# Six turns instead of eight for a head pair's attention, in a hybrid decoder layer on one core

## The chip, the cores and the metric

The kernel runs on one core of one Trainium2 chip. The metric is the device time of one execution in microseconds; the median of several runs is compared.

## The reference

One decoder layer for 1024 tokens of width 1024. The part that the change touches is the attention group: 8 heads of 64, "stick-breaking" attention, strictly causal.

```python
for blk in range(S // Q_BLOCK):              # eight tiles of 128 queries
    t0 = blk * Q_BLOCK
    L = t0 + Q_BLOCK                         # a tile looks at the keys before its end
    z = jnp.einsum('bhqd,bhkd->bhqk', qb, kb) * scale
    mask = s_idx < t_idx
    log_keep = jnp.where(mask, jax.nn.log_sigmoid(-z), 0.0)
    shifted = jnp.concatenate([log_keep[..., 1:], jnp.zeros_like(log_keep[..., :1])], axis=-1)
    suffix = lax.cumsum(shifted, axis=3, reverse=True)
    A = jnp.where(mask, jnp.exp(jax.nn.log_sigmoid(z) + suffix), 0.0)
    outs.append(jnp.einsum('bhqk,bhkd->bhqd', A, vb).astype(v.dtype))
```

Around it: an RMS norm and a projection to six blocks of 512 columns (b, c, h of a gated causal convolution, and q, k, v), a norm of q and k by head, a norm of both groups' outputs by head, the output projection, and a hierarchical mixture of 32 experts.

## The kernel before

Every engine has its own program, in which the order of all work is written out by hand, and semaphores join them.

Attention runs over four pairs of heads. For a pair the eight query tiles are gone through from the last (tile 7, 1024 keys) to the first (tile 0, 128 keys), one tile a *turn* for both heads: 32 turns, counted by n, and r is the turn within its pair. In iteration n of its loop (L495 to L509) TensorE does `scores(n + 1)`, `values(n - 1)`, `turn(n, 0)`, projection steps, `turn(n, 1)`, projection steps.

- `scores` (L442) multiplies q by k in three products of rounded and remaining parts into z, in banks 0 to 3 (two for each head, used in turn; `z_first`, `z_done` and the semaphore `z_read` say when one may be written again).
- ScalarE's `open_unit` (L587) reads z twice through a sigmoid: `kept` (1 - beta, L597) and `soft` (beta, L598).
- VectorE's `weigh` (L736) makes the running product of `kept` from the right with a scan (L744) and multiplies `soft` by it (L747).
- `turn` (L459) transposes `soft` in blocks of 128 into banks 4 and 5, ScalarE's `take_turned` (L600) copies these out to `probsT` (L606), and `values` (L469) multiplies them by v into bank 6, where four tiles share a bank that `take_values` (L609) copies out.

Between these, TensorE works off the projection of the chunks of columns of q, k, b, c and h, in *steps*: one matmul of 128x128 by 512 (L417). A group of 24 steps makes 512 tokens of one chunk. The first eight groups come ahead of attention; the others are handed out by `share(n)`, so many steps between the two heads' transposes and so many behind the second. All these groups are made in bank 7, and the first step of one waits until the group before has been read (L412). The readers are `take(g)` of ScalarE for k (a square L544 and a copy L545), of ScalarE and then VectorE for q (L549, L550 and L699), and of VectorE for c, h and b (L703, L708, L719). On VectorE `take` stands at the beginning of an iteration, for the groups that ended in the second part of turn n - 1 and the first of turn n, ahead of `weigh(n + 1, 0)`; on ScalarE at the beginning too, for the groups of turn n - 1. `chunk_lo` (L685) on VectorE makes the remaining part of the next weights.

In turn r = JOIN the pair stops for sums of squares: TensorE's `sums_of_qk` and `sums_of_rows` (L421, L435) write them to z banks, ScalarE changes its function table, takes logarithms and exponentials (`roots_of_qk`, `roots_of_rows`) and changes it back; one turn later VectorE scales with them (`scale_keys`, `keys_lo`, `scale_rows`).

Of the kernel before, what the change touches and what calls it, by code (L numbers as in the profile page):

```python
# [19 lines left out]
ALU = mybir.AluOpType  # L20
ACT = mybir.ActivationFunctionType
AX = mybir.AxisListType

P = 128
# [14 lines left out]

SHARE = ((8, 16),) * 8  # L40
SHARE_LAST = ((24, 24),) * 4 + ((0, 0),) * 4


def hymba_moe_layer(nc, x, norm_mix_w, w_in, conv_w, q_norm_w, k_norm_w, group_norm_conv_w,
# [33 lines left out]
    with ExitStack() as ctx:  # L78
# [162 lines left out]
        NPAIR = CB  # L241
        UNITS = NPAIR * NT
        PRE_GROUPS = 2 * PRE


        def share(n):
            return (SHARE if n < UNITS - NT else SHARE_LAST)[n % NT]

# [22 lines left out]
        for n in range(UNITS):  # L271
            z_first[n], z_before[n] = len(z_done), z_done[-1]
            z_done += [z_done[-1] + 2 * halves(n)] * halves(n)
            p, r = divmod(n - 1, NT)
# [10 lines left out]
        assert all(z_first[n] % 2 == 0 for n in range(UNITS) if halves(n) == 2)  # L285

# [9 lines left out]
        with nc.Block(no_gpsimd_drain=True) as block:  # L296
# [82 lines left out]
            def _(pe):  # L379
# [62 lines left out]
                def scores(n):  # L442

                    p, t = n // NT, tile_of(n)
                    cols = slice(t * P, (t + 1) * P)
                    if n % NT == 0:
                        pe.wait_ge(k_ready, p + 1)
                    q2, k2 = (q_hi[p % 2], q_lo[p % 2]), (k_hi[p % 2], k_lo[p % 2])
                    for hf in range(halves(n)):
                        c0, c1 = hf * BANK, min((hf + 1) * BANK, length(n))  # L450
                        pe.wait_ge(z_read, z_done[z_first[n] + hf - 2])
                        for i, (qs, ks) in enumerate(((0, 0), (0, 1), (1, 0))):
                            for h in range(2):
                                rows = slice(h * HD, (h + 1) * HD)
                                mm = pe.matmul(Z(z_first[n] + hf, h)[:, 0:c1 - c0], q2[qs][rows, cols], k2[ks][rows, c0:c1],
                                               start=(i == 0), stop=(i == 2))
                    mm.then_inc(scored, 1)

                def turn(n, h):  # L459
                    pe.wait_ge(weighed, 2 * n + h + 1)  # L460
                    for hf in range(halves(n)):
# [3 lines left out]
                        for j in range(4 * hf, min(4 * hf + 4, length(n) // P)):  # L465
                            mm = pe.transpose(TB(g)[:, (j % 4) * P:(j % 4 + 1) * P], soft[h][:, S - length(n) + j * P:S - length(n) + (j + 1) * P], ident)  # L466
                        mm.then_inc(turned, 1)

                def values(n):  # L469

                    p, t = n // NT, tile_of(n)
                    pe.wait_ge(turned_read, th(n + 1, 0))
                    if n == 0:
                        pe.wait_ge(bank_read[0], PRE)
                    elif n % 4 == 0:
                        pe.wait_ge(out_read, n // 4)
                    for j in range(t + 1):
                        for h in range(2):
                            head = slice((2 * p + h) * HD, (2 * p + h + 1) * HD)
                            mm = pe.matmul(ps[h * HD:(h + 1) * HD, VB, (t % 4) * P:(t % 4 + 1) * P], v[:, j, head], probsT[h][:, j, :],  # L480
                                           start=(j == 0), stop=(j == t))
                    mm.then_inc(valued, 1)
# [12 lines left out]
                for n in range(UNITS):  # L495
                    p, r = divmod(n, NT)
# [12 lines left out]
                    project(ticks_by(n, 1), ticks_by(n, 2))  # L509
# [3 lines left out]
            def _(act):  # L513
# [19 lines left out]
                def take(g):  # L533
# [7 lines left out]
                    if kind == "k":  # L541
                        if h == 0 and j >= 2:
                            act.wait_ge(scored, NT * (j - 1))
                        act.activation(k_sq[j % 2][:, half], o, ACT.Square).then_inc(k_squared, 1)  # L544
# [28 lines left out]
                def square_row(p, i):  # L573
# [3 lines left out]
                    if p == NPAIR - 1:  # L577
                        act.wait_ge(scored, NT * p)
                        act.wait_ge(k_scaled, NPAIR)
# [7 lines left out]
                def open_unit(n, h):  # L587
                    p, t, L = n // NT, tile_of(n), length(n)
                    act.wait_ge(scored, n + 1)
                    if n % NT == 0:  # L590
# [3 lines left out]
                    up, down = q_scale[p % 2][:, t, h:h + 1], q_minus[p % 2][:, t, h:h + 1]  # L594
                    b = 2 * h + z_first[n] % 2
                    z = psf[:, b * BANK:b * BANK + L]
                    act.activation(kept[h][:, S - L:], z, ACT.Sigmoid, scale=down).then_inc(kept_made, 1)  # L597
                    act.activation(soft[h][:, S - L:S - 1], z[:, 0:L - 1], ACT.Sigmoid, scale=up).then_inc(z_read, halves(n))  # L598

                def take_turned(n, h):  # L600
                    for hf in range(halves(n)):
# [3 lines left out]
                        k0, k1 = 4 * hf, min(4 * hf + 4, length(n) // P)  # L605
                        act.activation(probsT[h][:, k0:k1, :], TB(th(n, h) + hf)[:, 0:(k1 - k0) * P].rearrange("p (k t) -> p k t", t=P),  # L606
                                       ACT.Copy).then_inc(turned_read, 1)

                def take_values(i):  # L609

                    act.wait_ge(valued, 4 * i + 4)
                    if i == 2 * (NPAIR - 1):
# [26 lines left out]
                for n in range(UNITS):  # L639
                    p, r = divmod(n, NT)  # L640
                    if n:
# [6 lines left out]
                    for h in range(2):  # L648
                        take_turned(n, h)
                        if n + 1 < UNITS:  # L650
                            open_unit(n + 1, h)
                    if n and n % 4 == 0:
                        take_values(n // 4 - 1)
                    if r == JOIN[p]:
# [5 lines left out]
                        table(2)  # L660
                take_values(UNITS // 4 - 1)

            @block.vector
            def _(dve):
# [71 lines left out]
                def weigh(n, h):  # L736

                    L = length(n)
                    s, k, one = soft[h][:, S - L:], kept[h][:, S - L:], start_at[:, S - L:]
                    if n == 0:  # L740
                        dve.wait_ge(soft_ends, 2)
                    dve.wait_ge(kept_made, 2 * n + h + 1)
                    back = k[:, ::-1]
                    dve.tensor_tensor_scan(back, back, one[:, ::-1], 0.0, ALU.mult, ALU.max).then_inc(multiplied, 1)  # L744
                    dve.wait_ge(multiplied, 2 * n + h + 1)
# [38 lines left out]
                for n in range(UNITS):  # L784
                    p, r = divmod(n, NT)
                    if n:
# [806 lines left out]
```

## Time and profile before

| what | value |
| --- | --- |
| median of 3 runs | 1246.56 us (1245.02 to 1247.19) |
| the profiled execution | 1245.32 us, span 1243.6 us |
| TensorE matmul busy | 1114.1 us (90%) |
| TensorE weight load busy | 909.2 us (73%) |
| VectorE busy | 876.5 us (70%) |
| ScalarE busy | 723.9 us (58%) |
| GpSimd busy | 143.0 us (12%) |
| mean granted clock of TensorE | 0.946 of full speed |

Attention runs from 114.9 us (its first scores) to 445.5 us (the last copy of its values). Behind it come the output projection, the routing and, from 630 us, the experts. In the rows further on, a time is counted from the span's start, "x12" is the number of instructions merged into a row, and the brackets tell how long the engine was idle before and what ended that. PE is TensorE, DVE VectorE, ACT ScalarE.

### The profile page before, as it was taken

How to read it: one execution, taken by the hardware profiler on the slowest of the kernel's cores; microseconds unless marked ns; L12 is line 12 of the kernel's file. 1: busy time of each engine (PE TensorE's matmuls, PEld its weight loads, DVE VectorE, ACT ScalarE, POOL GpSimd, SP SyncE). 2: the span in 40 equal slices, each digit the busy share in tenths (PEclk: the TensorE clock that was granted, in tenths of full speed). 3: DMA queues.
4: the chain of work that ended last, by engine and by line, in shares of the span. 5: the costliest groups of instructions: out<-in, count | busy, mean ns of one | idle time of the engine just before them, and what ended most of it. 6: DMA issues, size and time to landing. Idle time of an engine off the chain costs nothing. (4 is left out here: it accounts for less than half of the span.)

```text
span 1243.6 us, 16698 instructions
## 1 busy us (share of the span) xinstructions
PE 1114.1 (90%) x5806; PEld 909.2 (73%) x5806; DVE 876.5 (70%) x918; ACT 723.9 (58%) x890; POOL 143.0 (12%) x193
## 2 busy tenths in 40 slices
PE   5998999999999869993589999999999999999920
PEld 4886777778778548883378888888888888888810
DVE  4405657576574563225579999999999999999816
ACT  4422655746633532111378888888888888888800
POOL 1001000000000310000101111111111111111000
PEclk9999999999999979995599999999999999999965
DMA  6111010110011362006279999999999999999219
GB/s 205 55 34 35 18 34 18 34 35 19 23 34 30 136 248 90 35 34 280 100 279 371 373 392 393 377 380 389 387 381 379 387 385 381 384 382 387 96 35 387
DMA packets 57338, 261.88 MB, mean 211 GB/s; under 512 B 13008, under 2 KB 33488, under 8 KB 43984
## 3 DMA queue, kind: packets, MB, share of 16 engines
q1 hardware_dynamic: 46928, 240.31, 50.7%
q0 software_dynamic: 9216, 16.80, 3.6%
q10 hardware_dynamic: 1152, 4.19, 0.8%
q8 instruction: 28, 0.46, 0.2%
q14 instruction: 14, 0.11, 0.0%
HBM read 252.88 MB, written 25.17 MB: 224 GB/s over the span
## 5 line engine op out<-in xcount | busy, mean ns | idle before, releaser
L1265 DVE TENSOR_TENSOR e_lo<-W,e_hi 128x1024 fp32r<-128x1024 f32 x384 | 452.6, 1221 | 25.8 <-ACT e_hi L1259 23.0
L1259 ACT ACTIVATE e_hi<-W 128x1024 fp32r<-128x1024 f32 x384 | 403.3, 1060 | 97.0 <-PE ps L1230 97.0
L1228 PE MATMUL ps<-e_hi,xT_hi 128*128 128x512 f32 x512 | 204.4, 399 | 7.1 <-DVE e_lo L1265 7.1
L1230 PE MATMUL ps<-e_lo,xT_hi 128*128 128x512 f32 x512 | 201.6, 394 | 0.0
L1229 PE MATMUL ps<-e_hi,xT_lo 128*128 128x512 f32 x512 | 201.0, 393 | 0.0
L744 DVE TENSOR_TENSOR_SCAN kept<-kept,start_at 128x1024 f32<-128x1024 f32 (+7 forms) x64 | 91.2, 1425 | 65.3 <-ACT kept L597 65.3
L417 PE MATMUL ps<-xnT_hi,w_hi 128*128 128x512 f32 x320 | 128.4, 401 | 2.4 <-DVE y_mix L719 0.9
L417 PE MATMUL ps<-xnT_hi,w_lo 128*128 128x512 f32 x320 | 128.1, 400 | 0.0
L417 PE MATMUL ps<-xnT_lo,w_hi 128*128 128x512 f32 x320 | 125.0, 391 | 0.0
L606 ACT ACTIVATE probsT<-ps 128x512 f32<-128x512 f32 (+3 forms) x96 | 43.8, 491 | 128.9 <-PE ps L466 128.8
L1228 PEld LDWEIGHTS ps<-e_hi,xT_hi 128*128 128x128 f32 x512 | 97.6, 191 | 27.0 <-issue 4.0
L1230 PEld LDWEIGHTS ps<-e_lo,xT_hi 128*128 128x128 f32 x512 | 97.0, 190 | 21.0
L1229 PEld LDWEIGHTS ps<-e_hi,xT_lo 128*128 128x128 f32 x512 | 97.4, 190 | 19.4
L1228 PE MATMUL ps<-e_hi,hidT_hi 128*128 128x512 f32 x256 | 103.1, 403 | 2.7 <-DVE e_lo L1265 2.7
L1230 PE MATMUL ps<-e_lo,hidT_hi 128*128 128x512 f32 x256 | 100.4, 392 | 0.0
L1229 PE MATMUL ps<-e_hi,hidT_lo 128*128 128x512 f32 x256 | 100.4, 392 | 0.0
L1322 POOL DMA_INDIRECT y_rows<-y,idx_pair x32 | 32.6, 1020 | 458.5 <-ACT y L1285 458.5
L417 PEld LDWEIGHTS ps<-xnT_hi,w_hi 128*128 128x128 f32 x320 | 60.5, 189 | 15.7 <-issue 3.6
L417 PEld LDWEIGHTS ps<-xnT_hi,w_lo 128*128 128x128 f32 x320 | 60.2, 188 | 13.1 <-issue 0.7
L417 PEld LDWEIGHTS ps<-xnT_lo,w_hi 128*128 128x128 f32 x320 | 60.3, 189 | 12.1 <-issue 0.2
L361 POOL CAST w_hi<-w_raw 128x1024 fp32r<-128x1024 f32 x20 | 23.5, 1176 | 320.6 <-DMA w_raw<-in_w_in_dram 320.6
L1228 PEld LDWEIGHTS ps<-e_hi,hidT_hi 128*128 128x128 f32 x256 | 48.6, 190 | 12.1 <-issue 2.9
(211 smaller groups left out, 1670.6 us busy)
## 6 DMA issues: line engine op xcount, KB each, us to landing
W<-in_w_dram SPq DMA_DIRECT2D x96, 2048.0 KB, 10.3
w_raw<-in_w_in_dram SPq DMA_DIRECT2D x20, 512.0 KB, 4.0
yy<-y_rows SPq DMA_DIRECT2D x8, 1024.0 KB, 13.5
xt<-in_x_dram SPq DMA_DIRECT2D x8, 512.0 KB, 3.7
w_out_raw<-in_w_out_dram SPq DMA_DIRECT2D x4, 1024.0 KB, 8.0
xn_rows<-xn SPq DMA_DIRECT2D x8, 512.0 KB, 2.6
out_dram<-x ACTq DMA_DIRECT2D x8, 512.0 KB, 8.9
x<-in_x_dram SPq DMA_DIRECT2D x1, 3072.0 KB, 14.9
```

The lines of the kernel that those rows point to most:

```text
L361: pool.tensor_copy(w_hi[c % 2], w_raw[c % 2]).then_inc(w_hi_made, 1)
L417: mm = pe.matmul(ps[:, group_bank(g)], w, r, start=(i % TICKS == 0), stop=(i % TICKS == TICKS - 1))
L606: act.activation(probsT[h][:, k0:k1, :], TB(th(n, h) + hf)[:, 0:(k1 - k0) * P].rearrange("p (k t) -> p k t", t=P), ACT.Copy).then_inc(turn ...
L744: dve.tensor_tensor_scan(back, back, one[:, ::-1], 0.0, ALU.mult, ALU.max).then_inc(multiplied, 1)
L1228: pe.matmul(o, xs_hi[:, k], e_hi[:, p, cols], start=(k == 0), stop=False)
L1229: pe.matmul(o, xs_lo[:, k], e_hi[:, p, cols], start=False, stop=False)
L1230: mm = pe.matmul(o, xs_hi[:, k], e_lo[:, p, cols], start=False, stop=(k == last))
L1259: act.activation(e_hi[:, p], flat[:, p * D:(p + 1) * D], ACT.Copy).then_inc(s["hi_made"], 1)
L1265: dve.tensor_tensor(e_lo[:, p], flat[:, p * D:(p + 1) * D], e_hi[:, p], ALU.subtract).then_inc(s["lo_made"], 1)
L1322: pool.indirect_dma_start(out=y_rows, out_offset=bass.IndirectOffsetOnAxis(ap=idx_pair[b].bitcast(U32), axis=0), in_=y[b], in_offset=None, ...
```

## The change

The constants and the turns. Tiles 7, 6, 5 and 4 keep a turn each; tiles 3 and 2 share one, and so do 1 and 0. A turn takes 12 + 20 projection steps in place of 8 + 16; in the last pair the first four turns take 24 + 24 and the others none, as before.

```diff
-SHARE = ((8, 16),) * 8
-SHARE_LAST = ((24, 24),) * 4 + ((0, 0),) * 4
+TURNS = ((7,), (6,), (5,), (4,), (3, 2), (1, 0))
+SHARE = ((12, 20),) * 6
+SHARE_LAST = ((24, 24),) * 4 + ((0, 0),) * 2
@@
-        UNITS = NPAIR * NT
+        NU = len(TURNS)
+        UNITS = NPAIR * NU
@@
-        JOIN = (4, 4, 4, 5)
-        tile_of = lambda n: NT - 1 - n % NT
-        length = lambda n: (tile_of(n) + 1) * P
-        halves = lambda n: (length(n) + BANK - 1) // BANK
+        JOIN = (3, 3, 3, 4)
+        tiles_of = lambda n: TURNS[n % NU]
+        length = lambda t: (t + 1) * P
+        halves = lambda n: 2
+        def parts(n):
+            tiles = tiles_of(n)
+            if len(tiles) == 1:
+                t = tiles[0]
+                return ((t, 0, BANK, S - length(t), 0), (t, BANK, length(t), S - length(t) + BANK, 4))
+            return ((tiles[0], 0, length(tiles[0]), S - length(tiles[0]), 0), (tiles[1], 0, length(tiles[1]), S - BANK - length(tiles[1]), 4))
```

`parts(n)` gives the two parts of a turn: the halves of one tile, or its two tiles. The second tile of a shared turn lies in the other z bank and in the lower half of `soft`, `kept` and `probsT`. `scores`, `turn`, `values` and `take_turned` go over these parts. ScalarE opens both tiles, the two `kept` first, and reads a group that ends in the first part of turn n between the two heads:

```diff
+                    for i, t in enumerate(tiles):
+                        end, L = S - i * BANK, length(t)
+                        b = 2 * h + (z_first[n] + i) % 2
+                        act.activation(kept[h][:, end - L:end], psf[:, b * BANK:b * BANK + L], ACT.Sigmoid,
+                                       scale=q_minus[p % 2][:, t, h:h + 1]).then_inc(kept_made, 1)
+                    for i, t in enumerate(tiles):
+                        end, L = S - i * BANK, length(t)
+                        b = 2 * h + (z_first[n] + i) % 2
+                        act.activation(soft[h][:, end - L:end - 1], psf[:, b * BANK:b * BANK + L - 1], ACT.Sigmoid,
+                                       scale=q_scale[p % 2][:, t, h:h + 1]).then_inc(z_read, 2 // len(tiles))
@@
                         take_turned(n, h)
                         if n + 1 < UNITS:
                             open_unit(n + 1, h)
-                    if n and n % 4 == 0:
-                        take_values(n // 4 - 1)
+                        if h == 0:
+                            for g in groups_in(n, 0):
+                                take(g)
+                    if n and r in (0, 4):
+                        take_values(2 * p + r // 4 - 1)
```

VectorE's `weigh` makes the scans of both tiles, clears the last column of the second tile and multiplies both. The order of its loop stays.

```diff
+                    for i, t in enumerate(tiles):
+                        end, L = S - i * BANK, length(t)
+                        dve.wait_ge(kept_made, scans(n, h) + i + 1)
+                        back = kept[h][:, end - L:end][:, ::-1]
+                        dve.tensor_tensor_scan(back, back, start_at[:, S - L:][:, ::-1], 0.0, ALU.mult, ALU.max).then_inc(multiplied, 1)
+                    dve.wait_ge(multiplied, scans(n, h) + len(tiles))
                     dve.wait_ge(z_read, z_reads(n, h))
-                    dve.tensor_tensor(s[:, :L - 1], s[:, :L - 1], k[:, 1:], ALU.mult).then_inc(weighed, 1)
+                    if len(tiles) == 2:
+                        dve.memset(soft[h][:, S - BANK - 1:S - BANK], 0.0)
+                    for i, t in enumerate(tiles):
+                        end, L = S - i * BANK, length(t)
+                        ins = dve.tensor_tensor(soft[h][:, end - L:end - 1], soft[h][:, end - L:end - 1], kept[h][:, end - L + 1:end], ALU.mult)
+                    ins.then_inc(weighed, 1)
```

All other lines of the diff put the new count of turns (NU for NT) into waits on `scored`, `valued` and `out_read`.

## Rows read from the trace of the kernel before

**Rows 1.** Granted TensorE clock in 40 slices of the span, in tenths, from the page.
```profile
PEclk9999999999999979995599999999999999999965
```
**Rows 2.** Busy time by stretch: start:end length, PE, PEld, DVE, ACT, POOL, clock, DMA share, GB/s.
```profile
132.88:207.71 74.83, 74.12 (x501) 58.76 (x501) 44.56 (x46) 41.53 (x73) 5.61 (x5) 1.00 0.10 29
365.27:417.80 52.53, 52.15 (x321) 42.00 (x320) 30.04 (x28) 18.43 (x31) 2.07 (x2) 1.00 0.07 21
417.80:449.67 31.87, 15.62 (x111) 9.10 (x111) 18.36 (x19) 21.23 (x36) 13.06 (x10) 0.79 0.43 158
```
**Rows 3.** Waits of TensorE's matmuls, 127 to 417 us: us in total, times, longest.
```profile
PE ps L417 <- DVE y_mix L719: 0.9, 2, 0.7
...
PE ps L466 <- DVE soft L747: 0.5, 1, 0.5
```
**Rows 4.** Timeline of TensorE in tile 1's turn: start us, us, engine, line.
```profile
183.67 0.48 PE L417 MATMUL ps<-xnT_hi,w_hi 128*128 128x512 f32 x1
...
185.61 0.38 PE L466 MATMUL ps<-start_at,soft 128*128 128x128 f32 x2
185.75 0.48 PE L417 MATMUL ps<-xnT_hi,w_lo 128*128 128x512 f32 x1
...
189.03 0.39 PE L417 MATMUL ps<-xnT_lo,w_hi 128*128 128x512 f32 x1
189.26 0.39 PE L417 MATMUL ps<-xnT_hi,w_lo 128*128 128x512 f32 x1
189.58 0.50 PE L455 MATMUL ps<-k_hi,q_hi 64*128 64x512 f32 x2
```
**Rows 5.** Timeline, first pair's second turn, from the second head's transposes on.
```profile
138.69 0.93 PE L466 MATMUL ps<-start_at,soft 128*128 128x128 f32 x7
...
139.37 0.47 PE L417 MATMUL ps<-xnT_hi,w_lo 128*128 128x512 f32 x1
...
140.97 0.92 ACT L598 ACTIVATE soft<-ps,q_scale 128x767 f32<-128x767 f32 x1
...
143.30 0.60 ACT L544 ACTIVATE k_sq<-ps 128x512 f32<-128x512 f32 x1 [1.41 <-PE ps L417]
...
143.80 0.59 ACT L545 ACTIVATE k_new<-ps 128x512 f32<-128x512 f32 x1
```
**Rows 6.** Timeline, VectorE's part in reading a query group.
```profile
229.17 0.69 DVE L699 TENSOR_TENSOR q_lo<-ps,q_hi 128x512 fp32r<-128x512 f32 x1 [0.23 <-ACT q_hi L550]
```
**Rows 7.** Timeline, a read of VectorE and the next group's first step.
```profile
380.60 0.69 DVE L703 COPY u<-ps 128x512 f32<-128x512 f32 x1 [7.53 <-PE ps L417]
...
381.34 0.50 PE L417 MATMUL ps<-xnT_hi,w_hi 128*128 128x512 f32 x1
```
**Rows 8.** Timeline, the last sigmoid ahead of the first pair's sums of squares.
```profile
168.02 0.58 ACT L598 ACTIVATE soft<-ps,q_scale 128x383 f32<-128x383 f32 x1
...
168.74 1.96 PE L433 MATMUL ps<-k_sq,same_head 128*128 128x512 f32 x4
```
**Rows 9.** Timeline of all engines in the tail, 423.5 to 445.2 us.
```profile
423.99 1.09 PE L480 MATMUL ps<-probsT,v 128*64 128x128 f32 x16 [2.65 <-ACT y_mix L615]
...
437.62 0.38 ACT L606 ACTIVATE probsT<-ps 128x256 f32<-128x256 f32 x1
...
438.97 1.28 DVE L734 SCALAR_TENSOR_TENSOR y_mix<-y_mix,gain_attn,k_new 128x1024 f32<-128x1024 f32 x1
...
442.55 0.42 DVE L744 TENSOR_TENSOR_SCAN kept<-kept,start_at 128x128 f32<-128x128 f32 x1
...
444.93 0.60 ACT L615 ACTIVATE y_mix<-ps 128x512 f32<-128x512 f32 x1 [0.79 <-PE ps L480]
```
**Rows 10.** Timeline of TensorE, its first matmul behind two idle times.
```profile
120.78 0.80 PE L455 MATMUL ps<-k_hi,q_hi 64*128 64x512 f32 x2 [4.22 <-ACT soft L598]
...
1184.48 0.76 PE L1228 MATMUL ps<-e_hi,hidT_hi 128*128 128x512 f32 x1 [2.73 <-DVE e_lo L1265]
```
**Rows 11.** Busy time by stretch, one behind the second of these idle times.
```profile
1184.20:1187.40 3.20, 2.92 (x7) 2.37 (x8) 3.20 (x4) 0.00 (x0) 1.31 (x2) 0.50 0.22 83
```

More of the change, by code:

```diff
@@ L241, in hymba_moe_layer @@
         NPAIR = CB
-        UNITS = NPAIR * NT
+        NU = len(TURNS)
+        UNITS = NPAIR * NU
+        assert sum(TURNS, ()) == tuple(range(NT - 1, -1, -1)) and all(t < 4 for tiles in TURNS for t in tiles[1:])
         PRE_GROUPS = 2 * PRE
         def share(n):
-            return (SHARE if n < UNITS - NT else SHARE_LAST)[n % NT]
+            return (SHARE if n < UNITS - NU else SHARE_LAST)[n % NU]
         def ticks_by(n, part):
@@ L273, in hymba_moe_layer @@
             z_done += [z_done[-1] + 2 * halves(n)] * halves(n)
-            p, r = divmod(n - 1, NT)
+            p, r = divmod(n - 1, NU)
             if n and r == JOIN[p]:
@@ L284, in hymba_moe_layer @@
         z_reads = lambda n, h: z_before[n] + (h + 1) * halves(n)
-        assert all(z_first[n] % 2 == 0 for n in range(UNITS) if halves(n) == 2)
+        assert all(z_first[n] % 2 == 0 for n in range(UNITS) if len(tiles_of(n)) == 1)
+        scans = lambda n, h: sum(2 * len(tiles_of(m)) for m in range(n)) + h * len(tiles_of(n))
         th = lambda n, h: sum(2 * halves(m) for m in range(n)) + h * halves(n)
@@ L442, in scores @@
                 def scores(n):
-                    p, t = n // NT, tile_of(n)
-                    cols = slice(t * P, (t + 1) * P)
-                    if n % NT == 0:
+                    p = n // NU
+                    if n % NU == 0:
                         pe.wait_ge(k_ready, p + 1)
                     q2, k2 = (q_hi[p % 2], q_lo[p % 2]), (k_hi[p % 2], k_lo[p % 2])
-                    for hf in range(halves(n)):
-                        c0, c1 = hf * BANK, min((hf + 1) * BANK, length(n))
+                    for hf, (t, c0, c1, at0, j0) in enumerate(parts(n)):
+                        cols = slice(t * P, (t + 1) * P)
                         pe.wait_ge(z_read, z_done[z_first[n] + hf - 2])
@@ L460, in turn @@
                     pe.wait_ge(weighed, 2 * n + h + 1)
-                    for hf in range(halves(n)):
+                    for hf, (t, c0, c1, at0, j0) in enumerate(parts(n)):
                         g = th(n, h) + hf
@@ L464, in turn @@
                             pe.wait_ge(turned_read, g - 1)
-                        for j in range(4 * hf, min(4 * hf + 4, length(n) // P)):
-                            mm = pe.transpose(TB(g)[:, (j % 4) * P:(j % 4 + 1) * P], soft[h][:, S - length(n) + j * P:S - length(n) + (j + 1) * P], ident)
+                        for j in range((c1 - c0) // P):
+                            mm = pe.transpose(TB(g)[:, j * P:(j + 1) * P], soft[h][:, at0 + j * P:at0 + (j + 1) * P], ident)
                         mm.then_inc(turned, 1)
                 def values(n):
-                    p, t = n // NT, tile_of(n)
+                    p, r = divmod(n, NU)
                     pe.wait_ge(turned_read, th(n + 1, 0))
@@ L474, in values @@
                         pe.wait_ge(bank_read[0], PRE)
[L475 to L481, printed above, removed]
+                    elif r in (0, 4):
+                        pe.wait_ge(out_read, 2 * p + r // 4)
+                    for i, t in enumerate(tiles_of(n)):
+                        for j in range(t + 1):
+                            for h in range(2):
+                                head = slice((2 * p + h) * HD, (2 * p + h + 1) * HD)
+                                mm = pe.matmul(ps[h * HD:(h + 1) * HD, VB, (t % 4) * P:(t % 4 + 1) * P], v[:, j, head], probsT[h][:, 4 * i + j, :],
+                                               start=(j == 0), stop=(j == t))
                     mm.then_inc(valued, 1)
@@ L495, in _ @@
                 for n in range(UNITS):
-                    p, r = divmod(n, NT)
+                    p, r = divmod(n, NU)
                     if n + 1 < UNITS:
@@ L542, in take @@
                         if h == 0 and j >= 2:
-                            act.wait_ge(scored, NT * (j - 1))
+                            act.wait_ge(scored, NU * (j - 1))
                         act.activation(k_sq[j % 2][:, half], o, ACT.Square).then_inc(k_squared, 1)
@@ L577, in square_row @@
                     if p == NPAIR - 1:
-                        act.wait_ge(scored, NT * p)
+                        act.wait_ge(scored, NU * p)
                         act.wait_ge(k_scaled, NPAIR)
@@ L587, in open_unit @@
                 def open_unit(n, h):
-                    p, t, L = n // NT, tile_of(n), length(n)
+                    p, tiles = n // NU, tiles_of(n)
                     act.wait_ge(scored, n + 1)
-                    if n % NT == 0:
+                    if n % NU == 0:
                         act.wait_ge(q_minus_made, p + 1)
@@ L593, in open_unit @@
                         act.wait_ge(turned, th(n - 1, h) + halves(n - 1))
[L594 to L598, printed above, removed]
+                    for i, t in enumerate(tiles):
[8 more added lines that the diff above has]
+                                       scale=q_scale[p % 2][:, t, h:h + 1]).then_inc(z_read, 2 // len(tiles))
                 def take_turned(n, h):
-                    for hf in range(halves(n)):
+                    for hf, (t, c0, c1, at0, j0) in enumerate(parts(n)):
                         act.wait_ge(turned, th(n, h) + hf + 1)
@@ L639, in _ @@
                 for n in range(UNITS):
-                    p, r = divmod(n, NT)
+                    p, r = divmod(n, NU)
                     if n:
@@ L660, in _ @@
                         table(2)
-                take_values(UNITS // 4 - 1)
+                take_values(2 * NPAIR - 1)
             @block.vector
@@ L736, in weigh @@
                 def weigh(n, h):
-                    L = length(n)
-                    s, k, one = soft[h][:, S - L:], kept[h][:, S - L:], start_at[:, S - L:]
+                    tiles = tiles_of(n)
                     if n == 0:
                         dve.wait_ge(soft_ends, 2)
[L742 to L745, printed above, removed]
-                    dve.wait_ge(z_read, z_reads(n, h))
-                    dve.tensor_tensor(s[:, :L - 1], s[:, :L - 1], k[:, 1:], ALU.mult).then_inc(weighed, 1)
+                    for i, t in enumerate(tiles):
[4 more added lines that the diff above has]
+                    dve.wait_ge(multiplied, scans(n, h) + len(tiles))
+                    dve.wait_ge(z_read, z_reads(n, h))
+                    if len(tiles) == 2:
[4 more added lines that the diff above has]
+                    ins.then_inc(weighed, 1)
                 dve.wait_ge(g1_in, 16)
@@ L784, in _ @@
                 for n in range(UNITS):
-                    p, r = divmod(n, NT)
+                    p, r = divmod(n, NU)
                     if n:
```

5 lines of the change are left out of this document (2 added, 3 removed).

## The prediction

> **What bounds the kernel now.** I read the page's slices first: apart from its two ends and the middle, TensorE is at 9 tenths at the full clock [rows 1]. The table by stretch then splits the attention stage by head pair: in the first pair TensorE is busy 74.12 of 74.83 us, in the last pair's four big tiles 52.15 of 52.53, but in the 31.87 us behind them only 15.62 [rows 2]. The waits say the same: between 127 and 417 us TensorE waits on L417 0.9 us for the largest releaser, and the four kinds of wait add up to 2.8 us [rows 3]. So three stretches matter: three pairs and most of a fourth that are bound by TensorE's own instructions, and a tail of 32 us that is bound by a chain through ScalarE and VectorE. What follows (projection out, routing, experts) is not touched.
>
> A change of the turns can therefore gain in the dense part only by fewer TensorE switches; it can gain in the tail; and it can lose wherever it makes TensorE wait. The last is what decides it.
>
> **What is the same.** All matmuls, transposes, activations and scans keep their number and sizes: a merged turn makes the scans of tiles 3 and 2 (or 1 and 0) one after the other. The 960 projection steps are also the same. Added are 16 one-column memsets on VectorE. No row shows one; the nearest is a scan over 128 columns, 0.42 us (442.55, [rows 9]), so each costs between 0 and 0.42. I take 0.1; they lie on a chain only for group 6 below.
>
> **Fewer turns in the dense part: a gain.** A step is repeated every 0.23 us (189.03 to 189.26). Eight steps take 1.94 us (183.67 to 185.61) and sixteen 3.83 (185.75 to 189.58) [rows 4], which is 8 and 16 times 0.227 and 0.12 and 0.20 over. So a change from one kind of work to another costs TensorE 0.1 to 0.2 us. A turn has six kinds of work in a row (scores, values, transposes, steps, transposes, steps), and for all but the transposes the change goes with the turn: 4 x 0.14, so I take 0.55 us for a turn removed, bounds 0.3 and 1.0. Two turns in each of three pairs: -3.3 us.
>
> **Where the groups of 24 steps end: the loss.** All groups from 8 on are made in one PSUM bank (group_bank gives 7), and the first step of a group waits until ScalarE or VectorE has read the bank of the group before. Before, a turn is 8 + 16 = 24 steps, so each group ends with its turn, and the next turn's scores, values and transposes hide the reading. Now a turn is 12 + 20 = 32 steps. The sums in a pair run 12, 32, 44, 64, 76, 96, 108, 128, 140, 160, 172, 192, and the groups end at 24, 48, 72, 96, 120, 144, 168, 192. Only 96 and 192 are ends of a turn. The six others lie inside a block of steps, with nothing between them and the next group. In the walk below X is the start of the transposes of the second head in the turn named.
>
> A bare VectorE read: the last step ends at 380.56, the copy runs 380.60 to 381.29 and TensorE goes on at 381.34 [rows 7]. So the next step starts 0.39 + 0.78 = 1.17 us after the last one did, in place of 0.23: 0.95 us. A key group (square, copy: 143.30 to 144.39, [rows 5]) costs in the same way 0.39 + 0.04 + 1.09 + 0.06 - 0.23 = 1.35. A query group has VectorE's subtraction behind the same two (229.17, 0.69 us and 0.1 behind ScalarE, [rows 6]): 0.39 + 0.04 + 1.88 + 0.06 - 0.23 = 2.15.
>
> - Group 1 (keys, ends 12 steps into the 20 of the first turn): ScalarE has done its turn by then, 1.35 (1.5 in later pairs, where the copy of the values comes first).
> - Group 2 (keys, 4 steps into the 20 of the second turn). ScalarE reads it only behind taking the transposes and opening the next unit. In this very turn before, X is 138.69, the second sigmoid ends at 141.89 = X + 3.2 [rows 5]; the group is read by X + 4.2. TensorE would go on at X + 0.68 (139.37) + 0.12 + 4 x 0.227 = X + 1.7. Loss 2.5.
> - Group 3 (queries, 8 steps into the 12 of the third turn): 2.15; ScalarE comes to it in time, 8 steps after the first head's transposes.
> - The sums of squares. They now follow a merged turn's opening, whose z uses two banks, and wait for its last reading. Before, only their second part (168.74) had to wait for the sigmoid of 168.02, which ended at 168.60, and the first part ran beside it [rows 8]. Now the whole opening counts. The nearest row is again [rows 5]: a copy of 896 columns and two sigmoids of 768 end at X + 3.2. Here it is a copy of 640, then 2 x 896 in two instructions more: about X + 3.5, where TensorE has only five transposes, 0.46. Loss 3.05, bounds 2 and 4.
> - Group 5 (VectorE's, 12 steps behind the sums): bare, 0.95.
> - Group 6 (VectorE's, 4 steps into the 20 of turn (3, 2)). VectorE must first finish weigh for turn (1, 0). It comes to it at about X + 2.2, behind keys_lo and chunk_lo (each as large as one scale_rows, 1.19 [rows 9]), of which the first starts when the first head's weigh is done, near X. Its sigmoids end at X + 2.85: those of [rows 5] less 2 x 384 columns at 0.9 ns (768 columns take 0.92, 384 take 0.58 [rows 8]) and two instructions more. A scan of 128 takes 0.42, so both take 1.2 and both products 0.8 with the memset: X + 4.2, and the read of 0.69 X + 4.9, where TensorE stands at X + 1.7. Loss 3.2; in the second and third pairs scale_rows lies ahead too, 2 x 1.19 (438.97 to 442.55 is three of them, [rows 9]): 5.6.
> - Group 7 (8 steps into the 12 of turn (1, 0)): bare, 0.95.
> - The group that ends the pair is now read in time, since the turn ahead of it has 12 + 20 steps: -0.66, the wait of before for L703 or L708, one per pair.
>
> First pair: 1.35 + 2.5 + 2.15 + 3.05 + 0.95 + 3.2 + 0.95 = 14.15, less 0.66: 13.5. The second and third have 0.15 + 2.4 more: 16.05 each. Together 45.6 us, and with the 3.3 us of fewer turns +42.3. Of the first pair's waits, 0.5 us of L466 for VectorE [rows 3] goes, since four more steps stand before it: +41.8. The fourth pair's 24 + 24 are kept, so its groups end with blocks as before.
>
> **The tail: a gain.** Counting from the last step's end at 417.8, the last copy starts at 444.93 and ends at 27.7 [rows 9]. Now, with the same durations set in the new order: the last group is read by 0.7, the last row squared by 1.9; four copies (0.4 to 0.6 each) and turn (1, 0)'s eight sigmoids (0.25 to 0.36 each from start to start) end at 7.0; the three rows' sums start there (two z banks again), and their logarithms, exponentials and the two tables take ScalarE to 17.4 (it was 437.62 - 417.8 = 19.8). Behind it stand only: two copies, the second head's three transposes, two copies, 12 values (0.9), one copy of 0.6. That ends at 20.7. The three scale_rows on VectorE, which stood ahead of the last weigh (438.97 to 442.55), now lie beside this. 27.7 - 20.7 = 7.0, less 0.5 for two tiles' scores ahead of the last steps: -6.5, bounds -4 and -9. Where the second block's first matmuls start sooner they may find a lower clock for longer; I keep that in the bounds.
>
> **The clock.** TensorE fell to 0.50 (1.2 GHz) after an idle of 4.22 us (matmul at 120.78, 0.80 us long in place of 0.50) and after one of 2.73 (at 1184.48), where 1184.20 to 1187.40 is at 0.50 [rows 10, 11]; an idle of 2.65 (at 423.99) was followed by 1.00 up to 424 and beyond [rows 1, 9]. The new idles of 3.05, 3.2 and 5.6 us are on the side that falls, those of 2.5 and 2.15 on the line or below it. I take two falls a pair. In 3.2 us at half clock about 3 us of dense work loses 1.5 us; the longer stretch after 120.78 lost about 2.5. Six falls at 1.7: +10 us, bounds 0 and 22. The Trainium skill, in "TensorE: Matmul & The Clock Gate" (HAM oscillation), says that a kernel whose matmul bursts are separated by waits is put back to half rate at each burst anew; by it every larger gap of a pair would be followed by a fall. The trace agrees behind 2.73 us (0.50, [rows 11]) and not behind 2.65.
>
> **Sum.** 41.8 - 6.5 + 10 = +45.3 us. The profiled execution took 1245.32 us (span 1243.6 and 1.7 around it), 1.24 below the median, so it would give 1290.6; against the median, 1292.
>
> **Rivals.**
> 1. No clock falls, the waits as walked: +35.3, 1282. For it: the idle of 2.65 us that did not fall. Chance 0.14.
> 2. The longer waits are covered, only the bare handoffs are paid: two keys 2.7, queries 2.15, three of VectorE's 2.85 are 7.7 a pair, less 0.66 and 1.1: 3 x 5.9 - 6.5 = +11, 1258. It needs ScalarE and VectorE to reach the reads earlier than their program order lets them; [rows 5] speak against it. Up to 1270: chance 0.10.
> 3. The clock falls at every wait over 2 us, and stays down longer: four or five falls a pair at 1.7 to 2.5 are 22 to 37 in place of 10: 1304 to 1319. Chance 0.08, since five such falls a pair would need the idles of 2.15 to fall where 2.65 did not. It is what the section of the Trainium skill named above would give.
> 4. The other side: the tail and the fewer turns win. They bring 6.5 + 3.3 + 2.0 (three times 0.66) = 11.8 us, 1235. This decides if the seven new waits of a pair cost under 3.9 us together, 0.56 each; the smallest read in the trace costs 0.95. It would hold if the groups' readers did not gate the next group, which the code's one bank excludes. Chance 0.02, and 0.02 for no change.
>
> **Numbers.** Forecast 1292 with its own 1285 to 1301: chance 0.64. The range reaches from 1270 to 1303; it leaves out rival 2, 3 and 4. What a measurement can tell from no change is about 0.2%, 2.5 us. Faster 0.02, same 0.02, slower 0.96.
>
> **What would show it.** In the changed trace the waits list TensorE's L417 waiting behind ScalarE's key copy and VectorE's reads, some 35 us more in three pairs, up to about 5 us at once; within a block of 12 or 20 steps a hole at the group's end; the matmul behind the sums' start waiting for a sigmoid; a table by pair with 11 to 20 us more for each of three pairs, the fourth's four tiles unchanged, a tail of 21 in place of 28 us; granted clock under 1.00 in each pair. It is wrong if the holes inside the blocks are missing, if they stay at a microsecond each (rival 2), or if the clock stays at 1.00 (rival 1).

## The result, and the profile after

The changed kernel takes 1299.81 us (median of 5 runs, 1298.29 to 1301.61) where the kernel before takes 1246.56: a ratio of 1.043 (95% interval 1.0415 to 1.0444), +53 us. The forecast was 1292 with a range from 1270 to 1303, slower. The two profiled spans are 1296.6 and 1243.6 us, so all of the difference can be read in them.

In the changed kernel a projection step is L429, the scores are L466, the transposes L477, the values L492, and the sums of squares L439 (queries) and L452 (rows). Of the readers, L556 and L557 are ScalarE's for keys, L718 is VectorE's part of a query group, and L722, L727 and L738 are VectorE's for c, h and b; L614 is ScalarE's sigmoid `soft`. In the variants with six turns these lines are up to ten further on.

The table by stretch first. In the changed kernel the stretches begin with the first scores behind TensorE's idle time of 4.22 us, with the end of the last projection step, and with the first matmul of the output projection (columns as in [rows 2]).

```profile
119.83:478.09 358.26, 316.12 (x1894) 246.32 (x1894) 182.26 (x196) 158.64 (x273) 18.55 (x17) 0.93 0.07 21
478.09:505.53 27.44, 15.61 (x105) 9.52 (x105) 14.82 (x19) 19.55 (x32) 11.43 (x10) 0.77 0.50 186
505.53:1296.60 791.07, 699.09 (x3330) 583.04 (x3330) 629.03 (x675) 501.11 (x520) 100.19 (x145) 0.93 0.78 302
```

The same three stretches of the kernel before:

```profile
120.78:417.80 297.02, 293.54 (x1888) 230.15 (x1888) 185.16 (x178) 158.19 (x269) 19.74 (x17) 0.99 0.09 26
...
449.67:1243.60 793.93, 701.75 (x3330) 584.93 (x3330) 629.09 (x675) 501.08 (x520) 100.26 (x145) 0.93 0.77 301
```

The dense stretch is 61.2 us longer: TensorE idles 42.1 us in it (358.26 - 316.12) where it idled 3.5, and it is busy 22.6 us longer with the same matmuls and six more (the scores of tile 2, which now stand ahead of the last steps and no longer in the tail). The tail answers [rows 2]'s third row: 27.44 in place of 31.87 us. What follows is 2.9 us shorter, though no line of it changed ("Outside the turns" below says why).

The waits of TensorE's matmuls between 127 and 475 us answer [rows 3]. All are new but 0.24 us of the last row, the fourth pair's wait at 472.34, which the kernel before has too:

```profile
PE ps L429 <- ACT k_new L557: 11.1, 6, 2.5
PE ps L439 <- ACT soft L614: 8.8, 3, 2.9
PE ps L429 <- DVE q_lo L718: 6.1, 3, 2.1
PE ps L429 <- DVE u L722: 5.7, 3, 4.2
PE ps L429 <- DVE u L727: 5.7, 3, 4.2
PE ps L429 <- DVE y_mix L738: 4.4, 4, 2.6
```

And the timeline of the first pair's second turn answers [rows 5], now with the hole inside a block of steps:

```profile
140.99 0.93 PE L477 MATMUL ps<-start_at,soft 128*128 128x128 f32 x7
...
142.45 0.40 PE L429 MATMUL ps<-xnT_hi,w_lo 128*128 128x512 f32 x1
...
143.27 0.91 ACT L614 ACTIVATE soft<-ps,q_scale 128x767 f32<-128x767 f32 x1
...
144.53 0.63 ACT L557 ACTIVATE k_new<-ps 128x512 f32<-128x512 f32 x1
...
145.30 0.76 PE L429 MATMUL ps<-xnT_hi,w_hi 128*128 128x512 f32 x1 [2.46 <-ACT k_new L557]
```

The key group ends with the fourth step of this block (142.45) and is read only behind ScalarE's second sigmoid; the next step follows at 145.30, and takes 0.76 us, at half clock. By stretch, the clock behind three of the first pair's holes:

```profile
144.90:148.20 3.30, 2.90 (x7) 2.35 (x8) 1.24 (x2) 0.26 (x1) 1.03 (x1) 0.50 0.36 107
158.60:161.80 3.20, 3.20 (x12) 2.63 (x11) 2.82 (x3) 1.02 (x3) 0.00 (x0) 0.50 0.00 0
175.60:182.30 6.70, 6.30 (x21) 4.79 (x21) 3.04 (x5) 2.50 (x4) 0.00 (x0) 0.50 0.00 0
```

Over the three pairs there are eleven such stretches, eight of 3.4 us and three of 6.8, 47.8 us together.

### The profile page after: what moved, and what is told of

The parts are those of the page before. It is cut to its first block and busy times, and to the rows that moved or that the text cites. A ratio compares the mean times of both kernels' runs of the same rounds, so it can differ in the third digit from the quotient of the medians.

```text
span 1296.6 us, 16650 instructions
## 1 busy us (share of the span) xinstructions
PE 1133.5 (87%) x5806; PEld 923.5 (71%) x5806; DVE 870.0 (67%) x934; ACT 722.7 (56%) x890; POOL 140.1 (11%) x193
## 5 line engine op out<-in xcount | busy, mean ns | idle before, releaser
L429 PE MATMUL ps<-xnT_hi,w_hi 128*128 128x512 f32 x320 | 134.6, 421 | 33.2 <-ACT k_new L557 11.1
L622 ACT ACTIVATE probsT<-ps 128x512 f32<-128x512 f32 (+1 forms) x96 | 42.1, 490 | 172.2 <-PE ps L477 172.2
L429 PE MATMUL ps<-xnT_lo,w_hi 128*128 128x512 f32 x320 | 130.2, 407 | 0.0
L429 PE MATMUL ps<-xnT_hi,w_lo 128*128 128x512 f32 x320 | 129.8, 406 | 0.0
L764 DVE TENSOR_TENSOR_SCAN kept<-kept,start_at 128x512 f32<-128x512 f32 (+5 forms) x64 | 86.1, 1366 | 55.8 <-ACT kept L609 55.8
L429 PEld LDWEIGHTS ps<-xnT_hi,w_hi 128*128 128x128 f32 x320 | 63.1, 197 | 54.7 <-issue 22.0
L429 PEld LDWEIGHTS ps<-xnT_lo,w_hi 128*128 128x128 f32 x320 | 62.9, 197 | 12.7 <-issue 1.0
L429 PEld LDWEIGHTS ps<-xnT_hi,w_lo 128*128 128x128 f32 x320 | 62.6, 196 | 13.0
L885 PE MATMUL ps<-w_out_hi,yT_hi 128*128 128x512 f32 x128 | 52.7, 412 | 5.1 <-DVE yT_lo L967 5.1
```

The costliest lines, as they stand in the source:

```text
L429: mm = pe.matmul(ps[:, group_bank(g)], w, r, start=(i % TICKS == 0), stop=(i % TICKS == TICKS - 1))
L622: act.activation(probsT[h][:, j0:j0 + (c1 - c0) // P, :], TB(th(n, h) + hf)[:, 0:c1 - c0].rearrange("p (k t) -> p k t", t=P), ACT.Copy).th ...
L764: dve.tensor_tensor_scan(back, back, start_at[:, S - L:][:, ::-1], 0.0, ALU.mult, ALU.max).then_inc(multiplied, 1)
L885: pe.matmul(o, yT_hi[m % 2][:, c], w_out_hi[:, c, cols], start=(c == 0), stop=False)
```

## The experiments

The theory: a group of 24 steps that ends inside a block of steps makes TensorE wait for its reader, and the idle time makes the clock fall, which costs as much again as half the waits. Its rivals: the merged turns bind by themselves; the excess over the forecast is wait and not clock.

**Aligned shares, e1_aligned.** Six turns as in the changed kernel, all groups ending where a block ends.

```diff
-SHARE = ((12, 20),) * 6
+SHARE = ((24, 24), (8, 16), (8, 16), (24, 24), (8, 16), (8, 16))
```

> Six turns, merged tiles, JOIN and tail as in the changed kernel; only the shares of projection steps differ: 24 + 24, 8 + 16, 8 + 16, 24 + 24, 8 + 16, 8 + 16, so that each group of 24 ends where a block of steps ends. Theory (the loss comes from groups that end inside a block): the six waits inside blocks go, with the clock falls behind them. What stays is the wait of the sums for the merged turn's opening, 2.9 us and one fall of about 2.5 us in each of three pairs (+16), a short wait for a key group behind 8 transposes (+1.5), the gain of fewer turns (-3.3) and the tail (-4.4): about 1256 us, range 1248 to 1264. Rival (merged turns themselves bind, their longer openings and scans): still above 1285 us, with waits of TensorE on transposes and scores.

Measured: 1259.55 us, ratio 1.011 (1.0066 to 1.0153), in the expected range. The two largest waits of its dense stretch are these. The sums' wait for the merged opening is as it was; the reads inside blocks are gone, and one wait of 1.9 us at a group's end between blocks has come:

```profile
PE ps L439 <- ACT soft L614: 8.8, 3, 2.9
PE ps L429 <- DVE y_mix L738: 2.1, 2, 1.9
```

So 40 of the 53 us hang on where the groups end, and not on the merging. The 13.7 us that are left go with the sums' wait and 20.5 us at half clock; e5 below takes them away.

**The groups' ends without the merging, e2_before_inside.** Eight turns; four of a pair's eight groups end 12 steps into a block.

```diff
-SHARE = ((8, 16),) * 8
+SHARE = ((12, 20), (8, 8)) * 4
```

> The kernel before, eight turns, nothing merged; only the shares of the first three pairs are 12 + 20 and 8 + 8 by turns, so that four of a pair's eight groups end 12 steps into a block of 20. Theory: waits of 1.2, 2.0, 0.8 and 0.8 us idle in each of three pairs (keys, queries, two reads of VectorE), 16 us in all, and a clock fall behind some of the 2.0: 1262 to 1270 us. Rival (the merging is the cause): within 3 us of 1246.6.

Measured: 1276.31 us, ratio 1.0247 (1.0218 to 1.0275). The merging is not needed for a loss. The size was missed by 6 us upwards. The twelve holes inside blocks make 14.9 us of idle time, near the 16 expected. Another 12.1 us I had not counted: TensorE idles 1.7 us at five ends that lie between blocks, and 0.5 to 0.7 us ahead of scores six times. That a turn of 8 + 8 steps is too short for what it has to cover is my reading of these; no run tests it. So this kernel's 30 us are not all due to groups that end inside blocks.

**Useless matmuls in the sums' wait, e3_fill.**

```diff
+        FILL = 9
@@
+                            pe.wait_ge(turned_read, th(n + 1, 0))
+                            for i in range(FILL):
+                                pe.matmul(TB(0), xnT_hi[:, 0, 0:P], xnT_hi[:, 0, 0:BANK], start=True, stop=True)
                             sums_of_qk(p + 1)
```

> The changed kernel, with nine useless 512-column matmuls (into a transpose bank that has been read) ahead of the sums of squares in the first three pairs, where TensorE idles 2.93 us. They take 2.0 us and nothing waits for them. Theory (the clock falls there and costs about 2.3 us each time, some 20 us over all eleven falls of the three pairs): the stretches of 6.8 us at half clock behind the sums' wait go, and the time falls by 5 to 8 us, to about 1293. Rival (the excess over the forecast is in the waits, not the clock): no change, 1299 to 1301.

Measured: 1291.80 us, ratio 1.0372 (1.0342 to 1.0403). The nine in the first pair:

```profile
174.57 2.33 PE L521 MATMUL ps<-xnT_hi 128*128 128x512 f32 x9 [0.74 <-ACT probsT L626]
```

The idle time is 0.74 in place of 2.93 us, and the three stretches of 6.8 us behind it are gone. Of 47.8 us at half clock 30.7 are left; among the other falls one went, one came and one became longer. No other wait went: useless work made the kernel 8 us faster.

**scale_rows a turn later, e4_rows_later.** In the second and third pair VectorE scales the rows in turn JOIN + 2, behind the reads of groups.

```diff
+                    if 0 < p < NPAIR - 1 and r == JOIN[p] + 2:
+                        scale_rows(p)
                     for g in groups_in(n, 0):
                         take(g)
@@
-                    if p and r == JOIN[p] + 1:
+                    if p == NPAIR - 1 and r == JOIN[p] + 1:
                         scale_rows(p)
```

> The changed kernel, with VectorE's scale_rows of the second and third pair one turn later, behind the reads of the groups of the turn before. Theory (the read of the group that ends in turn (3, 2) queues behind VectorE's own program): TensorE's idle time there falls from 4.16 us to the first pair's 2.6 in two pairs: -3.1 us, about 1296.5. Rival (the sigmoids of the merged turn are what it waits for): 4.16 stays, 1299.8.

Measured: 1300.75 us, ratio 1.0443 (1.0414 to 1.0472). In the trace the wait fell in both pairs from 4.16 to 2.57 us, as forecast:

```profile
299.56 0.47 PE L429 MATMUL ps<-xnT_hi,w_hi 128*128 128x512 f32 x1 [2.57 <-DVE u L727]
```

The time did not follow. This execution has 51.2 us at half clock in the pairs and 15.8 in the tail; the changed kernel, profiled beside the later runs, has 47.8 and 8.3. At 0.42 us each (below) that is 4.6 us against the 3.2 gained. The expected 1296.5 us were missed, and of the time alone the rival's 1299.8 was nearer. The queue theory holds for the wait; that the clock ate the gain is read from one execution each, and was not repeated.

**The key group read first, e6_key_read_first.** ScalarE reads the second half of a key chunk between taking the transposes and opening the next unit.

```diff
+        early = lambda g: CHUNKS[g // 2][0] == "k" and g % 2 == 1
@@
-                            take(g)
+                            if not early(g):
+                                take(g)
@@
                         take_turned(n, h)
+                        if h == 1:
+                            for g in groups_in(n, 1):
+                                if early(g):
+                                    take(g)
                         if n + 1 < UNITS:
                             open_unit(n + 1, h)
```

> The changed kernel, with ScalarE reading the second half of a key chunk ahead of opening the next unit's second head, not behind it. Theory (the 2.46 us idle in a pair's second turn is ScalarE's own order: two sigmoids stand before the read): the idle falls to a bare handoff of 1.2 us in three pairs, -3.8 us, and its clock falls mostly go: 1293 to 1296. Rival (the delayed opening is paid later by TensorE at the next transposes): 1299 to 1301.

Measured: 1290.71 us, ratio 1.0376 (1.0357 to 1.0395), 9.5 us under the changed kernel measured beside it (1300.21) and 2.3 us under the expected range. The hole of 2.46 us:

```profile
144.96 0.47 PE L430 MATMUL ps<-xnT_hi,w_hi 128*128 128x512 f32 x1 [1.26 <-ACT k_new L558]
```

It is a bare handoff now, 3.6 us less in three pairs, and the half-clock time is 34.1 us, 13.7 less, which at the price below is the other 6. The step behind the hole is at full clock (0.47). No other wait grew, so the delayed opening cost nothing.

**All three, e9_all_three.** The last three edits in one kernel; every group still ends where it does in the changed one.

> The changed kernel with the three edits together: nine useless matmuls ahead of the sums, the key group read ahead of the opening, scale_rows a turn later. All groups still end inside blocks. Theory (time = waits + 0.47 us for each us at half clock in the three pairs): idle time falls by 3 x 1.2 (keys) and 2 x 1.6 (rows), 6.8 us together; falls stay only behind the query group (2.05 us) and the group of turn (3, 2) (2.6), about 20 us at half clock in place of 47.6, -13 us: about 1280 us, range 1277 to 1284. Rival (the falls are not what costs): 1300.2 - 6.8 = 1293.

Measured: 1276.77 us, ratio 1.0247 (1.0220 to 1.0275). Just below the range of 1277 to 1284: three falls were left, 10.2 us at half clock and not 20, since three of its six holes of over 2 us were not followed by one.

The dense stretch of these kernels, from the first scores behind the 4.22 us to the last step, gives the clock's price. In order: changed kernel in a second execution, e3, e4, e6, e9.

```profile
121.93:481.50 359.57, 317.37 (x1894) 246.82 (x1894) 182.58 (x195) 158.80 (x273) 18.31 (x17) 0.93 0.07 21
120.58:471.98 351.40, 314.92 (x1921) 245.76 (x1921) 182.59 (x195) 158.59 (x273) 18.07 (x17) 0.95 0.07 22
121.17:479.19 358.02, 319.06 (x1894) 248.01 (x1894) 182.54 (x195) 158.59 (x273) 19.17 (x17) 0.92 0.07 21
120.51:469.28 348.77, 310.13 (x1894) 241.32 (x1894) 182.30 (x195) 159.35 (x273) 19.86 (x17) 0.94 0.08 22
121.70:456.81 335.11, 306.25 (x1921) 239.13 (x1921) 182.53 (x195) 159.16 (x273) 20.65 (x17) 0.98 0.08 23
```

A kernel with the same work and no fall in the pairs (e5, next) is busy 292.31 us. Off each row go 3.6 us, since at 21 waits the last matmul's end of 0.17 us stands alone, and for e3 and e9 the 27 useless matmuls, 6.1 us. Left are 21.5 us for 47.8 at half clock, 12.9 for 30.7, 23.2 for 51.2, 14.2 for 34.1 and 4.2 for 10.2: 0.41 to 0.45 us for each us at half clock in all five. One thing makes these a little low. Right behind the first scores every execution is at half clock for a while too: 6.8 us in e5 and e3, 5.1 to 6.0 in the other four. With that counted the five give 0.42 to 0.47. The changed kernel of the comparison gives 316.12 - 292.31 - 3.6 = 20.2 us in the same way, and 4.5 us at half clock behind its first scores where e5 has 6.8, worth another 1: about 21 us is what the clock costs it.

**Aligned, and the sums behind the steps, e5_sums_later.** The shares of e1, and the sums of squares behind the turn's last 24 steps.

```diff
                     turn(n, 1)
+                    project(ticks_by(n, 1), ticks_by(n, 2))
                     if r == JOIN[p]:
                         if p + 1 < NPAIR:
@@
                         if p:
                             sums_of_rows(p)
-                    project(ticks_by(n, 1), ticks_by(n, 2))
```

> Six turns with aligned shares (24 + 24, 8 + 16, 8 + 16, 24 + 24, 8 + 16, 8 + 16), and the sums of squares are made behind the turn's last 24 steps instead of ahead of them. Theory (what the aligned version still loses is the 2.93 us wait for the merged turn's opening in three pairs, with a fall of the clock behind it, against 8.8 + 7 us): the opening is over by then, the wait goes, and the kernel is faster than the one before: about 1243 us, range 1238 to 1249. Rival (the sums' results come too late for the next pair's keys, which wait for them): new waits of TensorE on k_lo of 3 us or more a pair, over 1252.

Measured: 1239.37 us, ratio 0.9955 (0.9942 to 0.9969): 0.45% faster than the kernel before, and 20 us faster than e1. Its stretches:

```profile
120.50:417.71 297.21, 292.31 (x1894) 232.50 (x1894) 182.15 (x195) 159.06 (x273) 19.46 (x18) 0.99 0.09 26
417.71:444.57 26.86, 14.93 (x105) 9.00 (x104) 14.85 (x19) 19.56 (x32) 11.45 (x10) 0.83 0.51 189
444.57:1235.80 791.23, 698.93 (x3330) 582.87 (x3330) 629.13 (x675) 501.19 (x520) 100.33 (x145) 0.93 0.78 302
```

With the groups' ends and the sums' wait out of the way nothing of the loss is left: those two, and the clock falls behind them, were all of it. The dense stretch is as long as before the change (297.21 against 297.02): TensorE is busy 1.2 us less in it and idle 1.4 us more. The tail is 5.0 us shorter. The other 2.7 us lie behind the tail and are the clock's, not the change's (see "Outside the turns"). The rival's wait for the next keys did not come.

**The sums' place in the last pair alone, e7_before_join4.**

```diff
-        JOIN = (4, 4, 4, 5)
+        JOIN = (4, 4, 4, 4)
```

> The kernel before, eight turns and 8 + 16 steps; only the last pair's sums of squares come one turn earlier (turn of tile 3 instead of tile 2), as the changed kernel has them too. It shows how much of the tail's gain is this and how much the two turns fewer. Theory (the gain is the turns that no longer stand behind ScalarE's tables and roots): three turns now stand behind them instead of two, no gain: 1246 to 1249 us. Rival (the earlier sums make the gain): 4 us less, 1242.

Measured: 1242.29 us, ratio 0.9977 (0.9967 to 0.9988): by the time alone, what the rival expected. The tail in its trace:

```profile
417.31:448.53 31.22, 16.55 (x110) 9.46 (x111) 15.96 (x19) 21.39 (x36) 11.94 (x10) 0.78 0.44 163
```

That is 0.65 us under the 31.87 of before. The eight executions with six turns have tails of 25.5 to 28.5 us, 3.4 to 6.4 under it, so by the traces the earlier sums make the small part and the two turns fewer the rest. But this execution is the slowest of ten (1245.52 us; the others took 1241.20 to 1245.03), and its last stretch is 1.3 us longer than that of the kernel before, which hides a part of the gain. And a part of the timed 2.9 us is the clock: seven executions of the kernel before with a mean granted clock of 0.947 have a median of 1243.83 us, six of this one with 0.947 have 1242.29, which leaves about 1.5 us. How the tail's gain divides is therefore shown only roughly.

**The changed kernel beside these, after_again.**

> The changed kernel itself, beside the others on the same chip, as what the variants of it are compared with: 1297 to 1302 us. The theory of the clock says that TensorE's idle times come out as before to 0.05 us, while the number of falls in the three pairs may differ by one or two.

Measured: 1300.21 us, ratio 1.0437 (1.0419 to 1.0455). TensorE's idle time in the dense stretch is 42.20 us against 42.14, and the falls are again eleven.

## Why the prediction was right, and where it was off

| term | forecast | measured |
| --- | --- | --- |
| waits inside blocks and ahead of the sums, less what went | +45.1 | +42.3 |
| fewer turns | -3.3 | -2.4 |
| the clock in the dense stretch | +10 | +21 |
| the tail, with tile 2's scores ahead of it | -6.5 | -3.9 |
| ahead of the first scores, and behind the tail | 0 | -3.8 |
| sum | +45.3 | +53 |

**The waits** are idle 42.14 - 3.48 and the 3.6 us of the matmuls' ends. The tail is 31.87 - 27.44, less 0.5 for the scores. The single waits came out within 0.15 us of the forecast, all but group 6's. Idle times in the first pair, and with the end of 0.17: 0.78 for VectorE's bare read (0.95, forecast 0.95), 1.18 for keys (1.35, forecast 1.35), 2.03 for queries (2.2, forecast 2.15), 2.46 for the key group behind the sigmoids (2.63, forecast 2.5), 2.93 for the sums (3.1, forecast 3.05). All seven waits of each pair are there, and no other came.

**Group 6 was mis-sized.** Forecast 3.2 and twice 5.6, measured 2.58 + 0.17 and twice 4.16 + 0.17: 3.0 us less in all, which makes up the difference in the first line of the table. The timeline of VectorE ahead of it, in the second pair:

```profile
293.01 1.22 DVE L748 TENSOR_TENSOR k_lo<-k_new,k_hi 128x1024 fp32r<-128x1024 f32 x1
...
294.14 1.28 DVE L753 SCALAR_TENSOR_TENSOR y_mix<-y_mix,gain_attn 128x1024 f32<-128x1024 f32 x1
...
295.34 1.28 DVE L753 SCALAR_TENSOR_TENSOR y_mix<-y_mix,gain_conv,conv_sq 128x1024 f32<-128x1024 f32 x1
...
296.54 1.00 DVE L764 TENSOR_TENSOR_SCAN kept<-kept,start_at 128x256 f32<-128x256 f32 x2
```

There is no chunk_lo between keys_lo (L748) and the rows (L753). In VectorE's loop it follows only a group that is the second half of a chunk, and the group that ended in the turn before (the prediction's group 5) is a first half. The prediction puts one there, at 1.19 us; in the two pairs with rows the miss is 1.27.

**The clock is the term that was half its size.** The step that failed is "two falls a pair", with idles of 2.15 and 2.5 us "on the line or below it". They fall nearly as often as the longer ones: eleven falls in three pairs of four larger holes each. The price of a fall was 1.7 us in the forecast and is 21 / 11 = 1.9. The prediction drew its line from one idle time of 2.65 us without a fall; one case was too little. Rival 3, with a chance of 0.08, was this mechanism, and its lower edge of 22 us for the clock is nearly what was measured. The Trainium skill's rule in "TensorE: Matmul & The Clock Gate" (HAM oscillation), that bursts separated by waits restart at the lower rate each time, was nearer to the traces than I took it: eleven of twelve here, though not where the holes were 1.3 us or less. The section tells it of waits longer than most of these, so the holes of 2.03 to 2.93 us fall outside its own example.

**Why the time still lay in the range.** The clock was 11 us too low and the tail 2.6 us too good; the waits were 2.8 us too high, and 3.8 us outside the turns were not in the sum at all. Without these last the same terms give 1303.6, over the bound of 1303. As far as one execution of each kernel shows, that the range held was in part luck.

**Fewer turns** were near the low end of their bounds. In e5, where the waits are short, TensorE is busy 1.2 us less than before over the whole stretch (292.31 against 293.54), though 0.5 us of scores came in, and though it was at half clock for 6.8 us at the start in place of 5.2, some 0.7 us: 2.4 us, or 0.4 for each of six turns and not 0.55. Four changes of work a turn at 0.14 was an estimate from step blocks alone. That the parts of a merged turn keep some of theirs is a guess.

**The tail** came out as ordered, but ScalarE leaves its tables at 19.3 us behind the last step and not at 17.4:

```profile
485.26 2.86 PE L452 MATMUL ps<-k_new,same_head 128*128 128x512 f32 x4 [2.78 <-ACT soft L614]
...
497.37 0.55 ACT L622 ACTIVATE probsT<-ps 128x256 f32<-128x256 f32 x2
```

The sums start at 7.17 (forecast 7.0), but behind an idle time of 2.78 us at half clock: 2.86 us for a row's four matmuls, where full clock takes 1.88. That is the same omission as in the pairs, though the prediction had it in the tail's bounds. The tail also differs between executions of the changed kernel: 27.44 us with 12.5 at half clock here, 26.52 with 8.3 in the second.

**Outside the turns** the span is 3.8 us shorter: 0.95 ahead of the first scores and 2.9 behind the tail. The first is scatter, since the second execution of the changed kernel starts its first scores at 121.93 where this one has 119.83. The last stretch takes 793.9 us in the kernel before, 795.3 in e7, 793.7 in e9, and 791.0 to 791.7 in all the others, the eight-turn e2 among them, so it is not the change. It is the clock again: the three long ones have 114.7, 116.0 and 114.4 us at half clock in this stretch, the eight others 108.3 to 109.0. A part of it can be seen at the second idle time of [rows 10]. It is 2.73 us long in all eleven executions, and in the same three the clock falls 0.4 to 0.7 us before its end. In the eight others it does not; the matmul behind it, 0.76 us long in the kernel before, takes 0.47 in the changed one:

```profile
1238.76 0.47 PE L1253 MATMUL ps<-e_hi,hidT_hi 128*128 128x512 f32 x1 [2.73 <-DVE e_lo L1290]
```

Why it falls in these three is open.

## What to carry to other kernels

When a quantum of work is dealt out differently, look where its units end before counting what is saved: the same 24-step group cost nothing where other work of the engine followed and 1 to 4 us where the next group followed in the same bank. Price an idle time of TensorE at full clock not by its length alone; from about 2 us on it mostly brought a fall, and a fall cost 1.9 us, nearly as much again; filling such a hole with useless matmuls paid. And read the one-turn-later readers' queues (ScalarE's openings, VectorE's scalings) in program order: moving one read ahead of two sigmoids was worth 9.5 us. The same merging that cost 53 us came out 0.45% under the kernel before once the groups ended with blocks and the sums stood behind the steps (e5).

## What the runs showed of the hardware

Of idle times of TensorE in the dense attention stretch of these eleven executions that began at full clock, none of 93 of 0.5 to 1.9 us was followed by a fall of the granted clock to half, 15 of 21 of 2.0 to 2.1 us were, 18 of 22 of 2.5 to 2.6 us, and every one of 15 of 2.9 us. Elsewhere the share was another: in the tail 7 of 8 of 2.8 us and one of two of 2.65 us were, and of the 2.73 us in the last stretch only 3 of 11. So the length alone does not decide. The same hole in the same program can go either way from one pair to the next: 2.46 us at 142.84 and 237.98 fell, at 338.18 it did not. A us at half clock in the dense stretch cost 0.42 to 0.47 us of TensorE's time. A one-column memset on VectorE took 0.06 us and lay beside a product.
